# Summing the first layer's later modulation columns on VectorE, and a mixture-of-experts router without broadcast rows

## What is computed

```
cond = silu(c)
mod = cond @ w_ada[layer] + b_ada[layer]        # 1024 -> 6144 = six groups of 1024 columns
shift_m, scale_m, gate_m, shift_f, scale_f, gate_f = split(mod, 6)
h = rms_norm(x, g) * (1 + scale_m) + shift_m
parts = split(h @ w_in[layer])                  # twelve slots of 256 columns
x = x + gate_m * (concat(conv, sgu, gla, hgrn of the parts) @ w_out[layer])
h = rms_norm(x, g2) * (1 + scale_f) + shift_f
x = x + gate_f * swiglu(h)                      # layer 0: 2816 wide
# layer 1 (first1): 8 experts, 3584 wide, the best two of each token
combine = sum(one_hot(top_idx) * softmax(top_val))
for e in range(8): out += combine[:, e] * swiglu_e(h)
```

## Time and profile before

| what | value |
|---|---|
| median of 3 runs | 2918.65 us (2912.33 to 2921.44) |
| the profiled execution | 2912.36 us |
| its span, first to last instruction | 2910.6 us |
| TensorE matmul busy | 2728.7 us, 94% |
| VectorE busy | 1531.6 us, 53% |
| ScalarE busy | 1057.5 us, 36% |
| GpSimd busy | 345.6 us, 12% |
| chain that ended last | TensorE 68%, issue 20%, GpSimd 7%, DMA 2%, VectorE 2% |
| mean granted TensorE clock | 0.949 of full speed |

### The profile page before, as it was taken

One profiled execution on the slowest core, in us unless ns is written; L12 is line 12 of the kernel. 1 busy time (PEld: TensorE's weight loads), 2 busy tenths in 40 slices (PEclk: granted clock), 3 DMA queues, 4 the chain that ended last, 5 costly groups with the idle time before them and its releaser, 6 DMA issues.

```text
span 2910.6 us, 36783 instructions
## 1 busy us (share of the span) xinstructions
PE 2728.7 (94%) x14102; PEld 2294.3 (79%) x14102; DVE 1531.6 (53%) x1601; ACT 1057.5 (36%) x1350; POOL 345.6 (12%) x99
## 2 busy tenths in 40 slices
PE   3999999998799999999999999977999999997999
PEld 2899899887577777777777776866799878886898
DVE  3420267433577777777777776344369434442212
ACT  1300222212465566666565564222222223331321
POOL 0000355100000000000000000010255100000553
PEclk9965999998899999999999999889999999998999
DMA  6334488332499999999999998120378433331442
GB/s 274 131 113 149 165 316 321 123 115 87 163 378 351 364 359 354 376 346 378 338 383 344 363 365 330 59 87 1 121 307 323 158 116 120 118 123 61 146 171 100
DMA packets 89517, 654.59 MB, mean 225 GB/s; under 512 B 9936, under 2 KB 9936, under 8 KB 9936
## 3 DMA queue, kind: packets, MB, share of 16 engines
q1 hardware_dynamic: 77472, 564.17, 51.7%
q10 hardware_dynamic: 11952, 89.12, 7.6%
HBM read 652.20 MB, written 1.05 MB: 224 GB/s over the span
## 4 chain that ended last, share of the span: by engine, by line
PE 68%; issue 20%; POOL 7%; DMA 2%; DVE 2%; ACT 1%; ACTq 0%; POOLq 0%; DVEq 0%; SPq 0%
PE bank L1077 67%; POOL ring_rounded L680 6%; DMA consts<-consts_dram 1%; DMA ring<-stream_dram 1%; PE bank L1551 1%; ACT work L986 0%; DVE work L1703 0%; DVE xT L1703 0%; DVE ring_rounded L1697 0%; ACT work L985 0%; DVE rstd L1756 0%; PE bank L1412 0%; DVE work L1718 0%; ACT down_high L843 0%; ACTq L699 0%
## 5 line engine op out<-in xcount | busy, mean ns | idle before, releaser
L1077 PE MATMUL bank<-proj_rounded 128*128 128x512 f32 (+1 forms) x1376 | 442.2, 361 | 0.0
L1077 PE MATMUL bank<-hT,ring 128*128 128x256 f32 x1856 | 423.5, 389 | 10.2 <-ACT hT L724 10.2
L1077 PEld LDWEIGHTS bank<-hT,ring 128*128 128x128 f32 x1856 | 361.1, 195 | 73.7 <-issue 23.7
L1077 PE MATMUL bank<-ring_rounded,proj_rounded 128*128 128x512 f32 x896 | 350.1, 391 | 0.0
L1077 PE MATMUL bank<-hT_rounded,proj_rounded 128*128 128x512 f32 x896 | 336.4, 436 | 7.0 <-DVE ring_rounded L1697 7.0
L1697 DVE TENSOR_TENSOR ring_rounded<-ring,hT_rounded 128x2048 fp32r<-128x2048 f32 x112 | 256.7, 2292 | 141.2 <-ACT hT_rounded L834 141.2
L1077 PEld LDWEIGHTS bank<-proj_rounded 128*128 128x128 f32 x1376 | 260.4, 189 | 33.5
L1077 PE MATMUL bank<-yT_rounded,ring_rounded 128*128 128x256 f32 x960 | 271.5, 283 | 0.0
L1703 DVE SCALAR_TENSOR_TENSOR work<-work,cond 128x2048 f32<-128x2048 f32 x72 | 268.1, 3757 | 4.8 <-DMA work<-stream_dram 4.5
L1697 DVE TENSOR_TENSOR ring_rounded<-ring,proj_rounded 128x2048 fp32r<-128x2048 f32 x112 | 256.6, 2291 | 2.3 <-ACT proj_rounded L834 0.5
L1077 PE MATMUL bank<-ff_hid,ring 128*128 128x256 f32 x1056 | 232.9, 379 | 0.0
(11 more groups left out here) (273 smaller groups left out, 3997.4 us busy)
## 6 DMA issues: line engine op xcount, KB each, us to landing
ring<-stream_dram SPq DMA_DIRECT2D x537, 1024.0 KB, 5.7
work<-stream_dram ACTq DMA_DIRECT2D x80, 1024.0 KB, 8.1
consts<-consts_dram ACTq DMA_DIRECT2D x1, 2209.0 KB, 35.0
params<-params_dram ACTq DMA_DIRECT2D x1, 1870.5 KB, 7.7
xT<-x_dram ACTq DMA_DIRECT2D x1, 1024.0 KB, 29.0
out_dram<-xT SPq DMA_DIRECT2D x1, 1024.0 KB, 3.9
```

Of the source, the lines that this page charges most:

```text
L1077: return pe.matmul(o, lhsT=a, rhs=b, start=start, stop=stop, skip_group_check=True)
```

## The change

Two things, independent of each other.

**First layer.** `modulate` is gone. The sixteen later slots are laid out like the lead's (2048 columns of 128 rows each: eight slots k=0..7 for the third and fourth group of 1024 columns, eight for the fifth and sixth) and are mixed with the projections' slots in the order `FIRST_ORDER`. `later_part`, called at eleven places of VectorE's `first_mixers`, takes the next such slot when it is there and adds it, times a column of `cond`, to one of two accumulators: `yT` for the first eight, the buffer `he` for the others. TensorE adds over the partitions with sixteen matmuls each: `sum_later(0)` behind `read_out(l, "g")`, `sum_later(1)` behind the last projection. SyncE's `load_first` waits for `mod_part` (VectorE) before it reuses the buffer of a later slot, and for `weights_used` before it reuses a projection's. All in one in-order queue.

**Router and experts.** No `comb_row` and `spot_row`: the spreading, the 32 matmuls, ScalarE's eight copies and one small matmul go. `comb` is finished in `combine_weights`, behind the first expert's first splits. ScalarE rounds the first two weight slots before it copies out the gathered tokens. In chunk 1 VectorE makes `back_pick` (tokens on partitions, two operations), in the last chunk of the same expert TensorE transposes it (two transposes more) and ScalarE copies it to `put_back`. The zeroing of `mod_acc` ahead of the experts goes; the first expert's three sums multiply instead of multiply and add.

The diff, cut to its core:

```diff
+FIRST_ORDER = [... for i in "0 1 m 2 m m 3 m 4 m m 5 m 6 m m 7 m m 8 m m 9 m m 10 m 11".split()]
+FIRST_AT = [FIRST_ORDER.index(s) for s in range(12)]
+LATER_AT = [i for i, s in enumerate(FIRST_ORDER) if s == "m"]
...
+            def load_first():
+                for n in range(FIRST_SLOTS + RING):
+                    if n >= RING:
+                        before = FIRST_ORDER[n - RING]
+                        if before == "m":
+                            sp.wait_ge(mod_part, KD + LATER_AT.index(n - RING) + 1)
+                        else:
+                            sp.wait_ge(weights_used, before + 1)
+                    sp.dma_start(ring[:, n % RING, :], stream_in[n]).then_inc(weights_here[n % RING], 16)
...
-                act.wait_ge(*moe_pe.at("rows", 0))
-                for b in range(4):
-                    act.activation(comb_row[...], bank(b)..., ACT.Copy)
-                    last = act.activation(spot_row[...], bank(4 + b)..., ACT.Copy)
-                last.then_inc(*moe_act.step("rows"))
...
+                        if c == EXPERT_CHUNKS - 1:
+                            if not is_first(e):
+                                act.wait_ge(m["scattered"], 2 * e)
+                            act.wait_ge(m["hid_low"], g + 1)
+                            act.activation(put_back, bank(4 + u, T, 2 * T), ACT.Copy).then_inc(m["backs"], 1)
...
-                evacuate_tokens(0)
                 for half in range(2):
                     high(half, 0, 0, 0, None)
+                evacuate_tokens(0)
...
+            def sum_later(part):
+                pe.wait_ge(mod_part, KD * (2 + part))
+                if part:
+                    sum_modulation(7, later_acc[1], 0, 1, 2 * KD).then_inc(weights_used, MOD_LATER)
+                    sum_modulation(7, later_acc[1], 1, 2 * KD, 2 * KD + 1).then_inc(*later_pe.step("b"))
+                else:
+                    sum_modulation(7, later_acc[0], 0, 2 * KD).then_inc(*later_pe.step("a"))
...
                 read_out(l, "g")
+                if n == 0:
+                    sum_later(0)
                 h_updates(l, 1)
...
                 project(n, [11], TOKEN_MAJOR, 2)
                 if n == 0:
-                    modulate(MOD_SLOTS - MOD_LEAD)
+                    sum_later(1)
...
-                mm(bank(5, 24, 25), const("before"), const("ones")[:, 0:1])
...
-                pe.wait_ge(*moe_vec.at("spread", 0))
-                pe.wait_ge(*moe_act.at("turned", 0))
-                for e in range(EXPERTS):
-                    for tt in range(NT):
-                        a = e % 2 * T + tt * P
-                        mm(bank(e // 2, a, a + P), comb_b[:, e, tt, :], const("ident"))
-                        last = mm(bank(4 + e // 2, a, a + P), spot_b[:, e, tt, :], const("ident"))
...
+                        if c == EXPERT_CHUNKS - 1:
+                            pe.wait_ge(m["back_picks"], e + 1)
+                            for j in range(NT):
+                                last = pe.transpose(bank(4 + u, T + j * P, T + j * P + P), back_pick[:, j, :],
+                                                    const("ident"))
...
+            def later_part(l, count=1):
+                if l:
+                    return
+                for _ in range(count):
+                    j = later_done[0]
+                    later_done[0] += 1
+                    acc, k, at = later_acc[j // KD], j % KD, LATER_AT[j]
+                    if j == 0:
+                        dve.wait_ge(*shift_act.at("h7", 0))
+                    dve.wait_ge(weights_here[at % RING], 16 * (at // RING + 1))
+                    if k == 0:
+                        last = ts(acc, ring[:, at % RING, :], cond_of(0)[:, 0:1], None, ALU.mult, ALU.bypass)
+                    else:
+                        dve.wait_ge(mod_part, KD + j)
+                        last = stt(acc, ring[:, at % RING, :], cond_of(0)[:, k:k + 1], acc, ALU.mult, ALU.add)
+                    last.then_inc(mod_part, 1)
...
-                else:
-                    dve.wait_ge(*moe_act.at("rows", 0))
-                    if next_layer < len(plan):
-                        mod_start(next_layer)
                 one_hot(0)
+                for half in range(2):
+                    low(half, 0, 0)
                 tokens_low(0)
-                for g in range(2):
-                    for half in range(2):
-                        low(half, 2 * g, g)
+                if not r:
+                    combine_weights()
+                for half in range(2):
+                    low(half, 2, 1)
```

More of the change, by code:

```diff
@@ L23 @@
 MOD_SLOTS = MODS * P // COLS
-MOD_LEAD = 2 * KD * P // COLS
 MOD_GROUP = 3
@@ L396, in build_program @@
         conv_vec = steps("conv_vec", "cv c0 c1 c2 y")
-        moe_pe = steps("moe_pe", "logits turned spots rows")
-        moe_act = steps("moe_act", "turned exp rows")
+        moe_pe = steps("moe_pe", "logits turned spots")
+        moe_act = steps("moe_act", "turned exp")
         moe_vec = steps("moe_vec", "copy max neg " + " ".join(f"gt{t} eq{t} low{t} sum{t} rk{t}" for t in range(NT)) +
-                        " sel pick den inv w spots spot most flag spread")
+                        " sel spots spot most flag pick den inv w")
         again_here = [sem(f"again_here{i}") for i in range(RING)]
@@ L1101, in project, with sum_modulation @@
                         pe.wait_ge(*proj_act.at("p", proj_before[n] + s - places))
[L1102 to L1118 removed]
+                    product(place[f"in{n}"] + s if n else FIRST_AT[s], bank(s % places), hT, s in token_major)
+            def sum_modulation(b, acc, first, end, to=0):
                 for t in range(first, end):
[L1121 removed]
+                    a = t - first + to
                     last = mm(bank(b, a, a + 1), acc[:, t * P:t * P + P], const("ones")[:, 0:1])
                 return last
[L1125 removed]
+            def sum_later(part):
[5 more added lines that the diff above has]
+                    sum_modulation(7, later_acc[0], 0, 2 * KD).then_inc(*later_pe.step("a"))
             def norm(n, which):
@@ L1549, in step @@
                             pe.wait_ge(m["hid_low"], g - 1)
+                        if c == 1 and not is_first(e):
+                            pe.wait_ge(m["backs"], e)
                         for j in range(2):
@@ L1901, in first_mixers @@
                 mask_scores(l, "h")
+                later_part(l)
                 states(l, "g", g_state, gdecay)
-                for f in range(2):
-                    states(l, f"h{f}", h_state[:, f, :, :], hdecay[:, f * NCH:f * NCH + NCH])
+                later_part(l, 2)
+                states(l, "h0", h_state[:, 0, :, :], hdecay[:, 0:NCH])
+                later_part(l, 2)
+                states(l, "h1", h_state[:, 1, :, :], hdecay[:, NCH:2 * NCH])
+                later_part(l)
                 here(CX)
@@ L1951, in router, with combine_weights @@
                 dve.wait_ge(*moe_vec.at("sel", 0))
+                dve.wait_ge(*moe_pe.at("spots", 0))
+                dve.tensor_copy(column, bank(5, P, 2 * P))
+                stt(spot, bank(5, 0, 16).rearrange("p (t e) -> p t e", t=NT), 1.0, rank, ALU.add, ALU.mult)\
+                    .then_inc(*moe_vec.step("spots"))
+                dve.wait_ge(*moe_vec.at("spots", 0))
+                ts(spot, spot, -1.0, None, ALU.add, ALU.bypass).then_inc(*moe_vec.step("spot"))
+                dve.tensor_reduce(most, bank(5, 16, 24), AX, ALU.max).then_inc(*moe_vec.step("most"))
+                dve.wait_ge(*moe_vec.at("most", 0))
+                ts(flag[:, :], most, float(P), None, ALU.is_gt, ALU.bypass).then_inc(*moe_vec.step("flag"))
+            def combine_weights():
                 dve.wait_ge(*moe_act.at("exp", 0))
@@ L2356, in lay_stream @@
     put(place["mod0"], wide_slots(at_mod[0])[::MOD_BLOCKS])
-    put(place["mod_rest"], column_slots(at_mod[0])[MOD_LEAD:])
+    later = wide_slots(at_mod[0]).reshape(KD, MOD_BLOCKS, P, SLOT)[:, 1:].transpose(1, 0, 2, 3).reshape(-1, P, SLOT)
+    for slot, to in zip(later, LATER_AT):
+        stream[to] = slot
     for n, kind in enumerate(plan):
```

96 lines of the change are left out of this document (43 added, 53 removed).

## The result

The changed kernel takes 2792.68 us (median of 4 runs, 2787.68 to 2796.35) against 2918.45 us for the kernel before on the same chip (2912.33 to 2921.44): 0.957 of its time, 95% interval 0.9549 to 0.9592, 125.8 us less. The forecast was 2793.0 us in a range of 2780 to 2812. The profiled execution took 2787.68 us with a span of 2785.9, so 124.7 us of span went.

The account below looks back on a forecast made before the run. TensorE's instruction list was taken to bound the first layer and the experts, an engine-to-engine chain the router. Terms -96.6 - 28.5 + 1.8 = -123.3 us gave 2789.1 profiled or 2795.4 timed; forecast 2793, range 2782 to 2812 (2780 with rivals).

Parts of the forecast that it names:

- First layer: Projections and mixers to output product: -105.8 + 8.1 + 1.2 - 1.1 + 1.0 = -96.6 us, bounds -101 to -86.5.
- The sums: First layer, TensorE: two sums of 32 instructions each, 4.5 and 3.6 us, together +8.1 (7.2 to 14.0).
- The loss behind the first sum: First layer: projection `p9` behind the first sum loses 0 to 2.3 us to a low clock, taken as +1.2.
- The ring: First layer's in-order slot loads: late parts stall TensorE before `p6`, +1.0 us (0 to 3.0); `p5` has 1 us margin.
- VectorE's lateness: First layer: sixteen parts, 39 us in 65 idle ones, covered where they stand, so 0 us.
- The output product: End of the first layer: wins back 0 to 2.3 us of clock loss, taken as -1.1; starts at 193 to 195.
- Router: Counts to first expert products: -27.5 for the chain, +0.5 for a gap, -1.5 for the clock; -28.5 (-25 to -29.5).
- The -1.5 for the clock: First expert products: TensorE idle 2 us instead of 5, so twelve instructions run faster, -1.5 us (0 to -1.8).
- Experts: Two transposes more in eight experts, 0.22 us a pair: +1.8 us, bounds 0 to +5.
- rival 2: First layer: clock stays low around both sums, +6 to +12 us, 2799 to 2805; chance 0.10.
- rivals 4 and 5: First layer: VectorE's 39 us of parts show, 2832 (chance 0.02); late parts block the queue, 2920 or more (0.02).
- Rival 1: First layer: late parts hold back projections in the in-order queue, starving TensorE 10 to 25 us, 2803 to 2818; chance 0.15.

Follow-up runs that it names:

- zeroing_kept: Changed kernel with the zeroing of the next modulation's accumulator kept ahead of the experts; one run 2809.11 us, logits to first expert product 27.92 us.
- tokens_first: Changed kernel with the old order: ScalarE copies out gathered tokens before rounding the first two weight slots, VectorE likewise; 2796.01 us in one run.
- gpsimd_behind_timed: Changed kernel with GpSimd's two pairs of masked copies waiting for VectorE's part pairs beside them; 2793.42 us, ratio 0.9572 to the kernel before.
- parts_twice: Changed kernel with VectorE doing each of the sixteen later parts twice; 2803.45 us, ratio 0.9632 to the kernel before, mixers 145.09 us.
- router_only: Kernel before with only the router's and experts' part of the change, first layer as before; 2888.37 us, ratio 0.9915 to the kernel before.
- both_sums_early: Changed kernel with the first sum moved behind projection 7 and the second ahead of the h heads' squares; 2796.92 us, ratio 0.958 to the kernel before.

## Why the prediction was right

The mechanism is right: both long stretches went where the forecast said they would, and each by its own half of the change. That the parts agree to a tenth is luck, since the same stages move by 1 to 2 us from profile to profile.

**First layer, -96.6 forecast, -96.6 measured** (-96.07 - 0.49). With the mixers of the other profiles of either first layer (128.1 to 130.0, and 224.2 or 225.5) the first number is -94.1 to -97.4. The terms:
- `modulate`: -105.8, as predicted; that all of it was on the path was the sure part.
- The sums: 3.73 + 3.83 = 7.6 against +8.1. The first stands behind small matmuls and still ran at the full level in this profile; in `zeroing_kept` and `tokens_first` the same sum took 4.99 and 5.18 us, the latter over the forecast's limit of 5.
- The loss behind the first sum: +1.2 forecast. The h1 update and `p9` lost 0.8 + 2.3 = 3.1 us. The read-outs behind `p9` took 1.1 less than before and `p10` 7.94 us instead of 8.45, having run partly at the half level before as well. Net +1.5. The middle value was right for the wrong reason: not half of the loss came, but the whole, and a part was given back.
- The ring: +1.0 forecast before `p6`, and none elsewhere. +0.5 measured, before `p5`. Two terms were off and cancelled: the parts beside GpSimd took 2.7 us each and not 3.7, and a load took longer to land. The row for the changed kernel's loads from 65 to 190 us, issue to landing, against 4.8 in the earlier trace rows:

```profile
DMA to landing us min/median/max: 4.7/6.1/9.3
```

  Part 2 ended at 85.82 + 5.59 = 91.4, and `p5` started 6.25 us later: the margin of 1 us was eaten by the landing. Over a load's way the median of the kernel before is no safe figure once the queue carries twice as much (DMA share 0.59 from 61 to 190 us). The single loads of the changed kernel up to 190 us say more. Those issued 3.5 us or more behind the one before took 4.7 to 5.3 us, and the seven issued 0.4 us behind another 6.8 to 8.7. The load for `p5` was issued at 91.44, 2.5 us behind one and 0.4 ahead of another, and took 6.1. In `gpsimd_behind_timed`, with neighbours 2.5 and 0.5 us away, it took 4.8, and TensorE didn't wait; why these two differ stays open.
- VectorE's lateness: 0, right (the parts stand at twelve places of `first_mixers`, not eleven), and `parts_twice` shows by how much: with each part doubled four waits came, all before 132 us.
- The output product: first slot 198.36 - 189.63 = 8.7 us against 9.2 before, so -0.5 of the -1.1 forecast. 3.8 us of thin work cost the product behind them nearly what 106 us had cost. It started at 189.6 and not at 193 to 195, as the first projection was 3.7 us earlier.

**Router, -28.5 forecast, -27.7 measured.** The chain to the first product was worked out as -27.5 and came as -27.7, with two terms off that cancel. The counts ended 1.1 us earlier and not 0.46, mostly by the clock (above). And from their end to the first product it took 9.85 us and not 9.45, as ScalarE began to round 2.2 us behind the counts and not 1.6. The +0.5 for the gap ahead of the zeroing was not needed (`zeroing_kept`). The -1.5 for the clock was wrong: from the first product to the one at 770.14 before it was 8.86 us, and now (636.87 to 645.70) 8.83. The first products again take 0.79 and 1.05 us, with a granted clock of 0.61 from 636.8 to 640.6 us against 0.57, though TensorE had been idle for 3 us and not for 5. A shorter idle time did not bring the clock back.

**Experts, +1.8 forecast, -0.3 measured** from the first product to the end. The chain of the changed kernel among the experts, an ordinary chunk and its transposes:

```profile
1391.79 0.22 PE bank L1557 x2
1392.00 8.60 PE bank L1096 x34
```

A chunk keeps its 8.82 us. The shortest distance from one expert's chunk with the scatter to the next went from 130.57 to 130.80 us, so 0.23 an expert, just the two transposes. But before, such distances varied up to 131.71, and now up to 132.02, and this variation covers the 1.8 us. The whole stretch to the end took 2149.0 us here and 2152.4 when the changed kernel was measured again, so the -0.3 says no more than that nothing large came. ScalarE's copy stands where it was put in the forecast:

```profile
769.96 0.39 ACT L883 ACTIVATE proj<-bank 128x256 f32<-128x256 f32 x1
770.59 0.39 ACT L864 ACTIVATE ff_silu<-bank 128x256 f32<-128x256 f32 x1 [0.24 <-PE bank L1096]
```

ScalarE still waits 0.24 us for TensorE behind it, so the copy costs nothing.

**What nobody forecast** and cancels: -3.7 us at the start and +3.6 between the second norm and the logits. The change edits neither. In the kernel before the sixteen matmuls ahead of the first projection took 6.52 us at granted clock 0.54, in the changed one 3.63 at 1.00; over all kernels run here the first projection starts between 61.2 and 65.7 us. `router_only`, whose first layer is the old one, starts it at 61.17, so this isn't the change's. The Trainium skill, "TensorE: Matmul & The Clock Gate", Part 1, says that how many matmuls run cold varies with the gate's phase from run to run; these rows agree. From the second norm to the logits `router_only`, with the old first layer, took 396.8 us, and the two profiles with GpSimd's copies behind the parts 392.9, so the +3.6 isn't the change's either. That these two cancel in the total is luck.

**The rivals.** The ring didn't starve TensorE (0.5 us), the loss behind the sums stayed under rival 2's +6, the experts' last chunk didn't stall, and nothing of rivals 4 and 5 came. Rival 1's mechanism exists: `parts_twice` brings it out at twice the length of a part.

## What to carry to other kernels

Work that one engine does alone with the others idle is worth its whole length, if its input can be had earlier and another engine has room; the check is one walk through that engine's queue and the in-order load queue, slot by slot, with the landing time of the busier queue and not of the present one. Thin TensorE work wasn't made cheaper by placing it: in the four places tried here it cost its own time at the full level and 2 to 4.5 us more, spread over itself, the small matmuls and the dense product behind it. In a chain that passes between idle engines take out whole links first (15.5 us here), then what stands at the head of a queue without being needed (6.0, and 1.9 for the weights), then put the independent work in the wait (2.5).

## What the runs showed of the hardware that was not expected

- A sum of 32 one-column instructions ran at granted clock 1.00 in 3.6 to 3.8 us, and the dense product behind it at 0.50 to 0.53 for its first 5 us, so the cost shows on work that is itself dense. In other profiles the sum itself was slower (4.21, 4.99, 5.18 and 5.69 us; granted 0.84 for the first of these), and the product then mostly lost less. From the sum's start to the next projection's end it took 15.9 us in the changed kernel, 15.9 with the sum behind projection 7, 15.5 in `both_sums_early`, and 17.3 both in `tokens_first` and in the timed version with GpSimd behind. At the full level throughout it would be an estimated 12.7 us (3.6 for the sum, 1.9 for the small matmuls, 7.2 for the product).
- VectorE and GpSimd side by side slow each other unequally: 2.7 to 2.8 us instead of 2.4 for a part of 128x2048, and 5.86 instead of 2.04 us for GpSimd's pair of 128x512 products.
- The 24 KB-a-partition zeroing was preceded by a gap of 1.23 us without a releaser, and the shorter instructions at the same place were not.
- A 1 MB load of the ring landed in 4.7 to 5.3 us when it was issued 3.5 us or more behind the one before, and in 6.8 to 8.7 us when 0.4 us behind it.
- Stretches in which nothing was edited vary from profile to profile: the first projection's start from 61.2 to 65.7 us, the mixers from 128.1 to 130.0, the way from the first expert product to the end from 2145.8 to 2156.1. Smaller differences of one profile say nothing, and only stretches between near landmarks told the edits apart. The new router's stretch stayed at 21.9 to 22.2 us.
